# The end of a fused encoder layer: blocks of 112, 112 and 96 tokens, a square and a gain on GpSimd, identities on TensorE

## What is computed

```python
gate = jax.nn.sigmoid(rmsnorm(h, g_ple) @ w_ple_gate)
h = h + (ple.astype(h.dtype) @ w_ple_proj) * gate
# then, at the end of reference()
y32 = x32 * lax.rsqrt(jnp.mean(x32 * x32, axis=-1, keepdims=True) + RMS_EPS)
y = (y32 * g_final)
```

## Time and profile before

| | |
|---|---|
| median of 3 runs | 1890.41 us (1890.31 to 1890.65) |
| profiled execution, device time | 1889.97 us |
| its span, first to last instruction | 1888.1 us |
| PE busy | 1877.4 us (99%) |
| DVE, ACT, POOL busy | 987.0, 711.2, 180.6 us |
| moved | 292.42 MB, mean 155 GB/s |

### The profile page before, as it was taken

One profiled execution on the slowest core, in us unless ns is written; L12 is line 12 of the kernel. 1 busy time (PEld: TensorE's weight loads), 2 busy tenths in 40 slices (PEclk: granted clock), 3 DMA queues, 4 the chain that ended last, 5 costly groups with the idle time before them and its releaser, 6 DMA issues.

```text
span 1888.1 us, 35125 instructions
## 1 busy us (share of the span) xinstructions
PE 1877.4 (99%) x12803; PEld 1873.6 (99%) x12803; DVE 987.0 (52%) x1505; ACT 711.2 (38%) x885; POOL 180.6 (10%) x280
## 2 busy tenths in 40 slices
PE   9999999999999999999999999999999999999998
PEld 9999999999999999999999999999999999999998
DVE  8766666664444444554444344434443444455554
ACT  6333333333333333334332333323333233333564
POOL 0111111110000000221000001000100000122121
PEclk9999999999999999999999999999999999999999
DMA  7555445435444444444444444444444444444442
GB/s 264 180 167 166 163 165 164 164 130 212 149 140 152 157 144 147 145 148 159 146 157 143 151 143 150 156 155 133 156 147 156 144 151 145 146 156 145 156 145 100
DMA packets 94310, 292.42 MB, mean 155 GB/s; under 512 B 13072, under 2 KB 26536, under 8 KB 94120
## 3 DMA queue, kind: packets, MB, share of 16 engines
q1 hardware_dynamic: 75760, 275.32, 44.6%
q10 hardware_dynamic: 18520, 16.69, 3.0%
HBM read 284.08 MB, written 9.46 MB: 155 GB/s over the span
## 4 chain that ended last, share of the span: by engine, by line
PE 99%; DVE 1%; DMA 0%; POOL 0%; ACT 0%; issue 0%; SPq 0%; POOLq 0%; ACTq 0%
PE banks L395 31%; PE banks L397 31%; PE banks L396 31%; PE banks L463 0%; PE banks L464 0%; PE banks L465 0%; PE banks L415 0%; PE banks L416 0%; PE banks L588 0%; PE banks L568 0%; PE banks L567 0%; PE banks L566 0%; PE banks L439 0%; DMA h<-in_x_t 0%; DVE v_rows L1015 0%; PE banks L438 0%
## 5 line engine op out<-in xcount | busy, mean ns | idle before, releaser
L628 ACT ACTIVATE w_hi<-w_raw 128x1024 fp32r<-128x1024 f32 x510 | 539.0, 1059 | 987.5 <-PE banks L397 980.8
L395 PE MATMUL banks<-x_hi,w_hi 128*128 128x320 f32 x2512 | 780.7, 311 | 0.0
L397 PE MATMUL banks<-x_hi,w_lo 128*128 128x320 f32 x2512 | 776.5, 309 | 0.0
L396 PE MATMUL banks<-x_lo,w_hi 128*128 128x320 f32 x2512 | 776.5, 309 | 0.0
L945 DVE TENSOR_TENSOR w_lo<-w_raw,w_hi 128x1024 fp32r<-128x1024 f32 x510 | 602.7, 1218 | 20.5 <-ACT w_hi L628 20.0
L396 PEld LDWEIGHTS banks<-x_lo,w_hi 128*128 128x128 f32 x2512 | 472.0, 188 | 0.2
L395 PEld LDWEIGHTS banks<-x_hi,w_hi 128*128 128x128 f32 x2512 | 472.0, 188 | 0.2
L397 PEld LDWEIGHTS banks<-x_hi,w_lo 128*128 128x128 f32 x2512 | 471.8, 188 | 0.0
L395 PE MATMUL banks<-o_hi,w_hi 128*128 128x320 f32 x1280 | 395.6, 309 | 0.0
L396 PE MATMUL banks<-o_lo,w_hi 128*128 128x320 f32 x1280 | 395.5, 309 | 0.0
L397 PE MATMUL banks<-o_hi,w_lo 128*128 128x320 f32 x1280 | 395.5, 309 | 0.0
(11 more groups left out here) (154 smaller groups left out, 1089.6 us busy)
## 6 DMA issues: line engine op xcount, KB each, us to landing
w_raw<-in_w_slabs SPq DMA_DIRECT2D x515, 512.0 KB, 4.0
out_kv_t<-k_t ACTq DMA_DIRECT2D x16, 160.0 KB, 2.7
out_kv_t<-v_t ACTq DMA_DIRECT2D x16, 160.0 KB, 2.9
h<-in_x_t ACTq DMA_DIRECT2D x1, 2560.0 KB, 9.6
out_y<-y_rows SPq DMA_DIRECT2D x4, 512.0 KB, 3.5
h<-in_x_t SPq DMA_DIRECT2D x3, 640.0 KB, 9.0
f_keys<-f_rows ACTq DMA_DIRECT2D x8, 224.0 KB, 4.1
bias_rows<-in_rel_rows ACTq DMA_DIRECT2D x1, 1024.0 KB
```

The lines of the kernel that those rows point to most:

```text
L395: nc.tensor.matmul(out, w_hi[:, slot, ws], hi[:, xs], start=k == lo_k, stop=False)
L396: nc.tensor.matmul(out, w_hi[:, slot, ws], lo[:, xs], start=False, stop=False)
L397: mm = nc.tensor.matmul(out, w_lo[:, slot, ws], hi[:, xs], start=False, stop=k == hi_k)
L628: nc.scalar.activation(w_hi[:, slot, :], w_raw[:, slot, :], ACT.Copy).then_inc(s_whi, 1)
```

## The change

- `Y_ROWS` becomes blocks of 112, 112 and 96 tokens, each turned from its own first token, each on the partitions from 0 up. The turned products load 112 or 96 columns, scalings work on 112 or 96 partitions, and the stores have 112, 112 and 96 rows.
- The two parts of the last gate block become 112 and 208 tokens (`token_part`) instead of 160 and 160.
- The square of the first part moves from DVE to GpSimd; the gain of the last block moves from ACT to GpSimd (a tensor_scalar instruction). Each has its own semaphore.
- The root and the inverse are taken in two instructions each: for the 112-row blocks, and for the 96-row block. The second inverse stands between DVE's first and second scaling.
- TensorE multiplies the identity by itself four times after the first of the three last sums, and seven times before it turns the fifth piece; the results go to the fifth bank of Y_BANKS and are never read.

```diff
-Y_ROWS = ((0, 0, P), (P, 0, P), (TOK - P, P - (TOK - 2 * P), TOK - 2 * P))
+Y_ROWS = ((0, 112), (112, 112), (224, 96))
...
-        def token_half(t, half):
-            return t[:, half * (TOK // 2):(half + 1) * (TOK // 2)]
+        def token_part(t, part):
+
+            return t[:, 0:Y_ROWS[0][1]] if part == 0 else t[:, Y_ROWS[1][0]:TOK]
...
-                sp.dma_start(io["y"][first + P - count if at else first:first + P, cols], src).then_inc(s_stored, 16)
+                sp.dma_start(io["y"][first:first + count, cols], src).then_inc(s_stored, 16)
...
-                    src = h[:, block * TOK + first:block * TOK + first + P]
-                    tr = nc.tensor.transpose(banks[:, Y_BANKS[n % len(Y_BANKS)], j * P:(j + 1) * P], src, ident[:, :])
+                    src = h[:, block * TOK + first:block * TOK + first + count]
+                    tr = nc.tensor.transpose(banks[0:count, Y_BANKS[n % len(Y_BANKS)], j * P:(j + 1) * P], src, ident[:, :])
...
-            for out, (first, at, count) in zip(row_sums, Y_ROWS):
-
-                pe.wait_ge(s_gated[3], 1 if first + P <= TOK // 2 else 2)
-                mm = nc.tensor.matmul(out, sq[:, first:first + P], ones[:, 0:1], start=False, stop=True)
+            def keep_busy(count):
+
+                for n in range(count):
+                    nc.tensor.transpose(banks[:, Y_BANKS[-1], 0:P], ident[:, :], ident[:, :])
+
+            pe.wait_ge(s_gated[0], 2)
+            for out, (first, count) in zip(row_sums, Y_ROWS):
+
+                if first == 0:
+                    pe.wait_ge(s_squared, 1)
+                else:
+                    pe.wait_ge(s_gated[3], 1)
+                mm = nc.tensor.matmul(out[0:count], sq[:, first:first + count], ones[:, 0:1], start=False, stop=True)
+                if first == 0:
+                    keep_busy(4)
             mm.then_inc(s_sum, 1)
             for n in range(ready_pieces, len(Y_PIECES)):
                 if n == len(Y_BANKS) - 1:
-
-                    pe.wait_ge(s_gated[0], 2)
+                    keep_busy(7)
...
-                    pe.wait_ge(s_hg, KB)
+                    pe.wait_ge(s_last_hg, 1)
...
-            act.wait_ge(s_gated[3], 2)
-            nc.scalar.activation(blk(h, KB - 1), blk(h, KB - 1), ACT.Copy, scale=gain(FINAL, KB - 1)).then_inc(s_hg, 1)
             act.wait_ge(s_sum, 4)
...
-            nc.scalar.activation(mean[:, 0:len(Y_ROWS)], sums, ACT.Sqrt, bias=eps[:, :], scale=1.0 / D_MODEL).then_inc(s_row_root, 1)
-            act.wait_ge(s_row_rstd, 1)
+            for part, count in ((slice(0, 2), Y_ROWS[0][1]), (slice(2, 3), Y_ROWS[2][1])):
+                sums = banks[0:count, SUM_BANKS[part.start]:SUM_BANKS[part.stop - 1] + 1, 0:1].rearrange("p b n -> p (b n)")
+                nc.scalar.activation(mean[0:count, part], sums, ACT.Sqrt, bias=eps[0:count, :], scale=1.0 / D_MODEL).then_inc(s_row_root, 1)
...
+            def invert_rows(number, part, count):
+
+                dve.wait_ge(s_row_root, number)
+                nc.vector.reciprocal(rstd[0:count, part], mean[0:count, part]).then_inc(s_row_rstd, 1)
+
+            invert_rows(1, slice(0, 2), Y_ROWS[0][1])
...
+                if n == 3:
+                    invert_rows(2, slice(2, 3), Y_ROWS[2][1])
...
+            last = blk(h, KB - 1)
+            pool.wait_ge(s_ssq, 3 * KB)
+            pool.wait_ge(s_plep, KB)
+            nc.gpsimd.tensor_tensor(token_part(sq, 0), token_part(last, 0), token_part(last, 0), ALU.mult).then_inc(s_squared, 1)
+            pool.wait_ge(s_squared, 1)
+            pool.wait_ge(s_gated[3], 1)
+            nc.gpsimd.tensor_scalar(last, last, gain(FINAL, KB - 1), None, ALU.mult).then_inc(s_last_hg, 1)
```

More of the change, by code:

```diff
@@ L254, in hybrid_layer @@
         s_gated = [sem(f"last_block_gated{i}") for i in range(4)]
+        s_squared = sem("last_block_first_part_squared")
+        s_last_hg = sem("last_block_gained")
         s_root = sem("root_ready")
@@ L293, in acc_count @@
             return t.count(1, add - (2 if t.first >= T_GATE else 0))
-        def token_half(t, half):
-            return t[:, half * (TOK // 2):(half + 1) * (TOK // 2)]
+        def token_part(t, part):
+            return t[:, 0:Y_ROWS[0][1]] if part == 0 else t[:, Y_ROWS[1][0]:TOK]
         def y_piece(n, at_bank):
             rows, group = Y_PIECES[n]
-            first, at, count = Y_ROWS[rows]
+            first, count = Y_ROWS[rows]
             cols = slice(group * Y_BLOCKS * P, (group + 1) * Y_BLOCKS * P)
             if at_bank:
-                return banks[at:at + count, Y_BANKS[n % len(Y_BANKS)], 0:Y_BLOCKS * P]
-            return y_rows[at:at + count, rows * D_MODEL + cols.start:rows * D_MODEL + cols.stop]
+                return banks[0:count, Y_BANKS[n % len(Y_BANKS)], 0:Y_BLOCKS * P]
+            return y_rows[0:count, rows * D_MODEL + cols.start:rows * D_MODEL + cols.stop]
         def by_engine(n, e):
@@ L356, in _ @@
                 rows, group = Y_PIECES[2 * pair]
-                first, at, count = Y_ROWS[rows]
+                first, count = Y_ROWS[rows]
                 cols = slice(group * Y_BLOCKS * P, (group + 2) * Y_BLOCKS * P)
-                src = y_rows[at:at + count, rows * D_MODEL + cols.start:rows * D_MODEL + cols.stop]
+                src = y_rows[0:count, rows * D_MODEL + cols.start:rows * D_MODEL + cols.stop]
                 sp.wait_ge(s_scaled[0], pair + 1)
                 sp.wait_ge(s_scaled[1], pair + 1)
-                sp.dma_start(io["y"][first + P - count if at else first:first + P, cols], src).then_inc(s_stored, 16)
+                sp.dma_start(io["y"][first:first + count, cols], src).then_inc(s_stored, 16)
             sp.wait_ge(s_stored, 16 * (len(Y_PIECES) // 2))
@@ L583, in turn_piece @@
                 rows, group = Y_PIECES[n]
-                first = Y_ROWS[rows][0]
+                first, count = Y_ROWS[rows]
                 for j in range(Y_BLOCKS):
                     block = group * Y_BLOCKS + j
-                    src = h[:, block * TOK + first:block * TOK + first + P]
-                    tr = nc.tensor.transpose(banks[:, Y_BANKS[n % len(Y_BANKS)], j * P:(j + 1) * P], src, ident[:, :])
+                    src = h[:, block * TOK + first:block * TOK + first + count]
+                    tr = nc.tensor.transpose(banks[0:count, Y_BANKS[n % len(Y_BANKS)], j * P:(j + 1) * P], src, ident[:, :])
                 tr.then_inc(s_turned_y, 1)
@@ L594, in _ @@
             row_sums = [banks[:, bank, 0:1] for bank in SUM_BANKS]
-            for out, (first, at, count) in zip(row_sums, Y_ROWS):
-                nc.tensor.matmul(out, ssq[:, first:first + P], ones[:, 0:1], start=True, stop=False)
+            for out, (first, count) in zip(row_sums, Y_ROWS):
+                nc.tensor.matmul(out[0:count], ssq[:, first:first + count], ones[:, 0:1], start=True, stop=False)
             pe.wait_ge(s_hg, KB - 1)
@@ L919, in _ @@
                 act.wait_ge(s_gated[0], part + 1)
-                nc.scalar.activation(token_half(tm(1), part), token_half(tm(0), part), ACT.Sigmoid).then_inc(s_gated[1], 1)
+                nc.scalar.activation(token_part(tm(1), part), token_part(tm(0), part), ACT.Sigmoid).then_inc(s_gated[1], 1)
             ready_root()
-            act.wait_ge(s_gated[3], 2)
-            nc.scalar.activation(blk(h, KB - 1), blk(h, KB - 1), ACT.Copy, scale=gain(FINAL, KB - 1)).then_inc(s_hg, 1)
             act.wait_ge(s_sum, 4)
-            sums = banks[:, SUM_BANKS[0]:SUM_BANKS[-1] + 1, 0:1].rearrange("p b n -> p (b n)")
-            nc.scalar.activation(mean[:, 0:len(Y_ROWS)], sums, ACT.Sqrt, bias=eps[:, :], scale=1.0 / D_MODEL).then_inc(s_row_root, 1)
-            act.wait_ge(s_row_rstd, 1)
+            for part, count in ((slice(0, 2), Y_ROWS[0][1]), (slice(2, 3), Y_ROWS[2][1])):
+                sums = banks[0:count, SUM_BANKS[part.start]:SUM_BANKS[part.stop - 1] + 1, 0:1].rearrange("p b n -> p (b n)")
+                nc.scalar.activation(mean[0:count, part], sums, ACT.Sqrt, bias=eps[0:count, :], scale=1.0 / D_MODEL).then_inc(s_row_root, 1)
             for n in range(0, len(Y_PIECES), 2):
                 rows = Y_PIECES[n][0]
-                first, at, count = Y_ROWS[rows]
+                count = Y_ROWS[rows][1]
+                act.wait_ge(s_row_rstd, 1 + rows // 2)
                 act.wait_ge(s_turned_y, n + 1)
-                nc.scalar.activation(y_piece(n, False), y_piece(n, True), ACT.Copy, scale=rstd[at:at + count, rows:rows + 1]).then_inc(s_scaled[0], 1)
+                nc.scalar.activation(y_piece(n, False), y_piece(n, True), ACT.Copy, scale=rstd[0:count, rows:rows + 1]).then_inc(s_scaled[0], 1)
             act.wait_ge(s_out, 16 * 3)
@@ L1286, in _ @@
             for part in range(2):
-                nc.vector.tensor_tensor(token_half(tm(0), part), token_half(acc, part), token_half(rstd, part), ALU.mult).then_inc(s_gated[0], 1)
```

(21 more changed lines are left out.)

## The result

The changed kernel takes 1893.44 us (median of 22 runs, 1891.42 to 1895.09), the kernel before 1890.40 us (22 runs, 1888.73 to 1892.07): a ratio of 1.0016, 95% interval 1.0010 to 1.0021. It is 3.0 us slower. That is less than the 0.2% that the chances went by, but the interval is clear of one, and the time lies above the stated range.

The account below looks back on a forecast made before the run. The store data queue was taken to bound the end: first store 0.06 us earlier and data 0.1 shorter gave a 1889.8 us profiled execution, plus 0.44 to the runs' median, stated as 1890.3 us, range 1889.9 to 1890.8.

Parts of the forecast that it names:

- What bounds the end: Last 4.9 us: set by a queue of store data; the full clock's gain worth 0.0 to 0.25 us at the end.
- the weak slice at 1883.0: Window of the old kernel's stores at 107 GB/s, taken as the only hold that earlier store issues could remove.
- The stores: Six final stores: 1.3 us each, 7.8 us of data against 7.9 before; slower bound 1.4 each, 8.4 us.
- Rival (3): Final stores collide at the same part of SBUF: 1.7 us a store, end 2.2 us later, 1892.6; chance 0.25.
- Rival (2): Final stores: time goes with rows, data 6.4 to 7 us, end 0.9 to 1.6 us earlier; chance 0.2.
- rival (4): Final stores: engines carrying a 112-row store are halved, 2.2 us a store, 12.8 in all, 1895.3; chance 0.02.
- The last block on DVE, the identities between the sums: Last block: DVE gains 0.4 us, four identities eat it; sums 0.06 us earlier (loss 0.1 to gain 0.15).
- The square on GpSimd: Last block, first part: takes 0.4 us (0.25 to 0.72), ready before TensorE comes; cost nothing, up to 0.1 us.
- The other price: Last block, second part: DVE's add may wait 0.25 to 0.7 us for GpSimd's square.
- The gain on GpSimd: Last block's scaling: about 1.2 us, ending near 1877.6, covered by over a microsecond.
- Two roots and inverses: Before the scalings: second scaling delayed 0.1 to 0.2 us, only store 2 waits; price 0 (0 to 0.1).
- The clock: During the turns: identities fill most of PE's rests; if full clock holds, store 6 is issued near 1882.5, not 1884.15.

Follow-up runs that it names:

- a_rows128: The changed kernel with the old row blocks (128, 128, and 64 on partitions 64 to 127), parts of 128 and 192 tokens; 1889.95 us against 1890.44, ratio 0.9999.
- the first kernel of stores alone: The whole layer left out, only stores of zeros in ten groups of six; six stores of 128 rows took 7.7 us of data, of 112 rows 9.5.
- b_rows112: The kernel before with only the blocks of 112, 112 and 96 rows and the root in two instructions; 1892.67 us against 1890.44, ratio 1.0015.
- a_nobusy: The changed kernel without its eleven products of identities; 1893.19 us against 1890.26, ratio 1.0015.

## Why the prediction was wrong, point by point

- **What bounds the end** was read rightly: the data queue, not the turns. With the clock at 1.00 in a_rows128 the end came 9.51 us after the first store, against 9.67 with the half clock: in these two profiles the full clock is worth 0.16 us, inside the 0.0 to 0.25 that were given. One reading was wrong: the weak slice at 1883.0 was taken for a hold that earlier issues could remove. It is there in a_rows128 too, whose stores are issued earlier, behind a slice with a share of 1.60. A share over 1 can only mean that a packet's whole time is counted where it starts; over both slices the share is 0.97, so no engine time was free (us; busy PE, granted clock, DMA share, GB/s):

```profile
1881.50:1882.00 0.50, 0.00 (x0) 1.00 1.60 229
1882.00:1882.50 0.50, 0.00 (x0) 1.00 0.33 123
```

- **The stores** are the step that failed. "I take the rows on both sides, 1.3 each" interpolated in the number of rows between 64 and 128, although the two stores had the same time for different reasons: in the bare stores a packet takes 160 ns with 128 rows, and 307 with 64 rows from partition 0 or 64. Neither row says what a block in between costs. Measured: 1.6 us for 112 rows (9.5 / 6), 1.4 for 96, 1.8 in the change's order (10.9 / 6) and 1.9 in the kernel (11.5 / 6). So the term "7.8 us against 7.9" was too low by 3.7 us, and its upper bound of 1.4 a store (8.4) by 3.1; that 10% for a "ragged run" came from no row.
- **Rival (3)** had the sign, and its point of decision of 1.33 us a store was passed. Its mechanism is shown in part: packets of these blocks are held up, alone and in a queue. That it is engines with seven rows meeting at one part of SBUF was argued, not shown. It got a chance of 0.25 and a price up to 2.2 us; the change cost 3.0. It was undersized since it took 1.7 us a store as its dearest case and knew no tail: in the kernel the data lasted 11.5 us, 1.9 a store.
- **Rival (2)** fell with the first kernel of stores alone, **rival (4)** with the rate: half the engines would show a share of 0.5, and it was 1.0.
- **The last block on DVE, the identities between the sums.** Forecast: sums 0.06 us earlier; measured 0.31. The first sum came a tenth earlier after the mark (2.26 us, before 2.36), and the last four instructions took 0.43 us, not 0.55. With 128 columns behind the identities (a_rows128) they took 0.50, with 112 and 96 but no identities (b_rows112) 0.53, before 0.62: both the narrower loads and the identities ahead of them shorten the group. The order was as forecast: the second square was ready at 1876.69, the sums had to wait for the identities until 1876.96.
- **The square on GpSimd** took 0.37 us (0.4 forecast) and its result was there at 1876.04, before TensorE came for it at 1876.36. It cost nothing. The other price, a DVE add held by 0.25 to 0.7 us, was oversized: it was held by about 0.06, see the end.
- **The gain on GpSimd** took 1.09 us, forecast 1.2, and was covered. **Two roots and inverses**: the second store was not late.
- **The clock** held, as forecast, but the runs without identities show that it need not have fallen without them. The issues did not gain from it: store 6 was to be issued 1.7 us earlier, and came 10.67 us after the mark (at 1884.77), before 10.68, as store 5's issue was held for 2.68 us.

## What to carry to other kernels

Before a transfer's shape is changed, ask which partitions it covers and not how many rows it has: 64 rows from partition 32 went out in half the time of 64 rows from 0 or 64, and 112 or 96 rows from 0 took longer than 128. When the DMA queue sets the end, stages ahead of it can only move its start, and an engine's clock behind it is worth nothing. And where neither neighbour of a new shape explains the other's price, a kernel of bare stores gives it in one run; interpolation does not.

## What the runs showed of the hardware that was not expected

- A store of 112 rows takes longer than one of 128, alone (0.44 us more) as in a queue (0.3 more); one of 96 0.36 and 0.1 more. Queued, 96, 112 and 120 rows exceed the 7.7 us of 128 rows (7.9 to 9.5), and 48, 64 and 80 don't by more than 0.1. Why single packets of these blocks are held up is open: the trace does not say which engine carries which row, and the side of the memory that is written was not varied.
- The order of the sizes counts more than that they are mixed. 112 and 96 in turn took 8.7 us, no more than three of each by themselves, (9.5 + 8.4) / 2 = 8.9; 128 and 112 in turn 9.0, by themselves 8.6; four of 112 and then two of 96 took 9.4, by themselves (4 x 9.5 + 2 x 8.4) / 6 = 9.1; 112, 112, 96 twice took 10.9 and 10.5. Of the 1.1 to 1.5 us between these two orders, about 0.5 is slower packets (a mean of 8.5 and 8.4 us of packets on each engine, against 8.0), the rest a longer wait for the last engines.
- A thin tail ends the groups with 112 or 96 rows. In the 112-row group the share is 0.58, 0.30, 0.18 and 0.06 in the four half microseconds from 25.0; in the mixed one a single engine works for the last 1.5 us:

```profile
90.00:90.50 0.50, 1.00 0.04 16
90.50:91.00 0.50, 1.00 0.08 33
91.00:91.50 0.50, 1.00 0.06 25
```

- The issue of a store can itself be held while the queue ahead of it is long: 2.68 us for store 5 of the changed kernel, 2.46 in b_rows112, 2.59 in a_nobusy. Whether the tail comes from this was not tried.
- DVE waited for GpSimd, but hardly. GpSimd's square (1875.67 to 1876.04) lay under the end of DVE's multiply and the first part of DVE's add:

```profile
1875.44 0.37 DVE L1305 TENSOR_TENSOR tmp<-tmp,ple_part 128x208 f32<-128x208 f32 x1
1875.85 0.43 DVE L1307 TENSOR_TENSOR h<-h,tmp 128x208 f32<-128x208 f32 x1
1876.31 0.38 DVE L1312 TENSOR_TENSOR sq<-h 128x208 f32<-128x208 f32 x1
```

The add took 0.43 us where its neighbours of the same width took 0.37 and 0.38, and it ended 0.24 us behind the square. Line 961 ends 0.35 us behind GpSimd's instruction with 320 columns, and each of its 32 turns in the loop starts within 13 ns of such an instruction; 208 of 320 of that is 0.23. In a_rows128 the add has 192 columns, takes 0.46 us where its neighbours take 0.35 and 0.36, and ends 0.22 us behind the square, where 192 of 320 gives 0.21. So these rows fit an add that reads only once GpSimd is done, with most of its wait hidden in the add's own start. The Trainium skill, SBUF — State Buffer, section Who interferes with whom, has the two exclude each other for a whole instruction; the rows agree with that, and the forecast of 0.25 to 0.7 us missed how much of the wait is hidden.
